# The first stage of a streaming encoder layer, reordered by token tile and weight quarter

## The reference, cut to what matters

```
xn = x * rsqrt(mean(x * x) + EPS) * g_mix_norm
z = xn @ w_in                       # 1024 x 3488
c_q, c_kv, k_r, u, gate_a, gate_b = split(z)   # 256 + 128 + 32 + 1024 + 1024 + 1024 columns
```

## Time and profile before

| | |
|---|---|
| median of three runs | 859.44 us (859.42 to 859.92) |
| the profiled execution | 859.77 us |
| its span | 857.5 us |
| TensorE busy | 841.3 us, 98% |
| VectorE, ScalarE, POOL busy | 572.4, 365.2, 199.1 us |
| first transpose, first latent product, item 0 (starts) | 5.38, 15.12, 39.49 us |

### The profile page before, as it was taken

How to read it: one execution, slowest core, us unless ns; L and a number is a source line. 1 busy time by engine, 2 the same in 40 slices (tenths; PEclk the granted TensorE clock), 3 DMA queues, 4 the chain that set the end, 5 groups by cost and what they waited for, 6 DMA issues and landing times.

```text
span 857.5 us, 16853 instructions
## 1 busy us (share of the span) xinstructions
PE 841.3 (98%) x6564; PEld 806.9 (94%) x6564; DVE 572.4 (67%) x1056; ACT 365.2 (43%) x608; POOL 199.1 (23%) x228
## 2 busy tenths in 40 slices
PE   7999999899999999999999999999999999999998
PEld 7999899789999899877999999999999999999998
DVE  5686678877676676887655888878888886222121
ACT  6635959755645556557245222222222221222121
POOL 4021123202111121121140444333442344010000
PEclk9999999999999999999999999999999999999999
DMA  8434211131120200100223233232323223233321
GB/s 256 112 91 109 78 51 39 40 81 38 33 58 18 53 26 28 50 2 26 75 75 99 74 99 92 79 98 73 98 79 92 86 79 93 83 106 103 105 57 40
DMA packets 114466, 63.73 MB, mean 74 GB/s; under 512 B 7660, under 2 KB 112878, under 8 KB 114412
## 3 DMA queue, kind: packets, MB, share of 16 engines
q1 hardware_dynamic: 112428, 59.25, 24.2%
q0 software_dynamic: 1936, 3.70, 1.7%
q10 hardware_dynamic: 48, 0.02, 0.0%
HBM read 59.85 MB, written 2.70 MB: 73 GB/s over the span
## 4 chain that ended last, share of the span: by engine, by line
PE 88%; ACT 6%; DVE 3%; issue 2%; DMA 0%; SPq 0%; ACTq 0%; DVEq 0%
PE PS L1632 49%; PE PS L1785 9%; PE PS L1868 6%; PE PS L1840 4%; PE PS L1802 4%; PE PS L1678 3%; PE PS L1744 2%; PE PS L1822 2%; PE PS L2075 2%; PE PS L1776 2%; PE PS L1740 1%; PE PS L1766 1%; PE PS L1707 1%; PE PS L1644 1%; PE PS L1847 1%
## 5 line engine op out<-in xcount | busy, mean ns | idle before, releaser
L682 ACT ACTIVATE w_hi<-w_raw 128x1024 fp32r<-128x1024 f32 (+2 forms) x102 | 105.4, 1034 | 301.4 <-PE PS L1632 288.8
L1115 DVE TENSOR_TENSOR w_lo<-w_raw,w_hi 128x1024 fp32r<-128x1024 f32 (+2 forms) x102 | 127.2, 1247 | 103.6 <-ACT w_hi L682 103.5
L1632 PE MATMUL PS<-x2h,w_hi 128*128 128x272 f32 x704 | 145.7, 288 | 0.0
L1632 PE MATMUL PS<-x2h,w_lo 128*128 128x272 f32 x704 | 145.7, 288 | 0.0
L1632 PE MATMUL PS<-x2l,w_hi 128*128 128x272 f32 x704 | 145.1, 288 | 0.0
L1632 PEld LDWEIGHTS PS<-x2h,w_hi 128*128 128x128 f32 x704 | 110.8, 188 | 0.1
L1632 PEld LDWEIGHTS PS<-x2l,w_hi 128*128 128x128 f32 x704 | 110.6, 189 | 0.0
L1632 PEld LDWEIGHTS PS<-x2h,w_lo 128*128 128x128 f32 x704 | 109.9, 189 | 0.0
L643 POOL TENSOR_TENSOR uct<-uct 128x512 f32<-128x512 f32 x22 | 28.4, 1292 | 165.0 <-DVE uct L1585 165.0
L1632 PE MATMUL PS<-hh,w_hi 128*128 128x272 f32 x308 | 64.2, 289 | 0.0
L1632 PE MATMUL PS<-hh,w_lo 128*128 128x272 f32 x308 | 63.8, 288 | 0.0
(11 more groups left out here) (295 smaller groups left out, 1865.1 us busy)
## 6 DMA issues: line engine op xcount, KB each, us to landing
w_raw<-in_w_up_dram SPq DMA_DIRECT2D x44, 512.0 KB, 3.8
w_raw<-in_w_in_dram SPq DMA_DIRECT2D x24, 512.0 KB, 3.8
w_raw<-in_w_down_dram SPq DMA_DIRECT2D x16, 512.0 KB, 3.6
w_raw<-in_w_out_dram SPq DMA_DIRECT2D x8, 512.0 KB, 3.6
w_raw<-in_w_down_dram SPq DMA_DIRECT2D x8, 384.0 KB, 3.9
xnat<-in_x_prompt_dram SPq DMA_DIRECT2D x4, 512.0 KB, 5.0
w_raw<-in_w_in_dram SPq DMA_DIRECT2D x4, 416.0 KB, 6.5
wq<-in_w_q_b_dram SPq DMA_DIRECT2D x8, 192.0 KB, 2.5
```

Of the source, the lines that this page charges most:

```text
L682: nc.scalar.activation(hi[:, slot % 2, 0:n], raw[:, slot % 4, 0:n], ACT.Copy).then_inc(s_hi, 1)
L1115: tt(lo[:, slot % 2, 0:n], raw[:, slot % 4, 0:n], hi[:, slot % 2, 0:n].bitcast(F32), ALU.subtract).then_inc(s_lo, 1)
L1632: last = mm(joined_half(2 * rank, j), w[:, slot % 2, cols], x[:, k0 + k, j * HT:(j + 1) * HT], start=(k0 + k == 0 and first), stop=(k0 + k ...
```

## The change

The tokens go through the first stage in seven parts (`XPARTS`): tiles 0 and 1 in halves of four feature blocks, the others whole. SP loads them so, with the four weight quarters between, and the small vectors behind all of them. For each part VectorE scales the transposed columns by the gain from PSUM into a buffer `xg` (`x_scaled`), ScalarE makes the high part from it (`x_hi`), VectorE the low part (`x_lo`). ScalarE copies each transposed tile to `xT` on its own (`x_kept`). The latent weight quarters are split into places of their own, `lw_hi` and `lw_lo`. TensorE's order is written out: transposes, latent products by tile and quarter (`latent_product`, six matmuls) and ten identity products in three groups. Tiles 1 and 3 are transposed into banks 6 and 7, the others into 0 and 1; tiles 3 and 4 accumulate in banks 6 and 7, so their first products also wait for the kept copy of tile 3. The splits of items 0 and 1 stand ahead of ScalarE's vector copy and exponential, and ahead of VectorE's softplus chain; the copy of `rsT` stands behind that chain.

```diff
+        xg = at("xg", [P, 2, KD, P], gates_at)
+        lw_hi = at("lw_hi", [P, 4, 2 * LAT], v_at + 4 * 2 * P * 4, F32R)
+        lw_lo = at("lw_lo", [P, 4, 2 * LAT], gates_at + 2 * KD * P * 4, F32R)
...
+        XPARTS = [(0, 0, 4), (0, 4, 8), (1, 0, 4), (1, 4, 8)] + [(t, 0, 8) for t in range(2, NTT)]
+        def parts_of(t):
+            return sum(part[0] <= t for part in XPARTS)
+        def part_with(t, k):
+            return [k0 <= k < k1 and tile == t for tile, k0, k1 in XPARTS].index(True)
+        def x_columns(t, k0, k1):
+            bank = 6 if t in (1, 3) else 0
+            return PS[:, bank:bank + 2, :].rearrange("p a (k n) -> p (a k) n", k=4)[:, k0:k1, 0:TOK[t][2]]
+        def x_tile(x, t, k0, k1):
+            c0, _, n = TOK[t]
+            return x[:, k0:k1, c0:c0 + n]
...
-            for t, (c0, p0, n) in enumerate(TOK):
-                src = i["x_prompt"][0, c0:c0 + n, :] if t < NT else i["x_sample"][0]
-                sp.dma_start(xnat[p0:, t, :], src).then_inc(s_xt[t], 16)
+            def load_x(t, d0=0, d1=D):
+                c0, p0, n = TOK[t]
+                src = i["x_prompt"][0, c0:c0 + n, d0:d1] if t < NT else i["x_sample"][0]
+                sp.dma_start(xnat[p0:, t, d0:d1], src).then_inc(s_xt[part_with(t, d1 // P - 1)], 16)
             def latent_weights(t):
                 sp.dma_start(raw[:, t, 0:2 * LAT].rearrange("p (k n) -> p k n", k=2),
                              w_in_k[:, 2 * t:2 * t + 2, 0:LAT]).then_inc(s_w[t], 16)
+            load_x(0, 0, D // 2)
             latent_weights(0)
+            load_x(0, D // 2, D)
+            load_x(1, 0, D // 2)
+            load_x(1, D // 2, D)
             latent_weights(1)
+            load_x(2)
+            latent_weights(2)
+            load_x(3)
+            load_x(4)
+            latent_weights(3)
...
-            latent_weights(2)
-            latent_weights(3)
...
-            pool.wait_ge(s_xt[NT], 16)
+            pool.wait_ge(s_xt[-1], 16)
...
-                if not isinstance(t, int) or t >= 2:
+                if not isinstance(t, int) or t >= I_IN + 2:
...
+            def x_hi(part):
+                t, k0, k1 = XPARTS[part]
+                act.wait_ge(s_xg, part + 1)
+                nc.scalar.activation(x_tile(xnh, t, k0, k1), xg[:, t % 2, k0:k1, 0:TOK[t][2]], ACT.Copy).then_inc(s_xgh, 1)
+            def x_kept(t):
+                act.wait_ge(s_xTd, parts_of(t))
+                nc.scalar.activation(x_tile(xT, t, 0, KD), x_columns(t, 0, KD), ACT.Copy).then_inc(s_xTa, 1)
+            def latent_split_hi(q):
+                act.wait_ge(s_w[q], 16)
+                nc.scalar.activation(lw_hi[:, q, :], raw[:, q, 0:2 * LAT], ACT.Copy).then_inc(s_hi, 1)
+            def squares(t):
+                _, p0, _ = TOK[t]
                 if t:
                     act.wait_ge(s_ss, t)
                 nc.scalar.activation(junk[p0:, :], xnat[p0:, t, :], ACT.Square, accum_out=small[p0:, 2, t:t + 1]).then_inc(s_ss, 1)
...
+            act.wait_ge(s_vecT, 1)
+            nc.scalar.activation(vec[:, 0:8], PS[:, 2, 0:8], ACT.Copy).then_inc(s_vec, 1)
+            x_hi(0)
+            latent_split_hi(0)
+            x_hi(1)
+            x_hi(2)
+            latent_split_hi(1)
+            x_hi(3)
+            x_kept(0)
+            x_kept(1)
+            x_hi(4)
+            latent_split_hi(2)
+            act.wait_ge(s_cpre, 1)
+            squares(0)
+            x_kept(2)
+            x_hi(5)
+            squares(1)
+            x_kept(3)
+            x_hi(6)
+            x_kept(4)
+            latent_split_hi(3)
+            for t in range(2, NTT):
+                squares(t)
+            split_hi(I_IN, I_IN, 32)
+            split_hi(I_IN + 1, I_IN + 1, 32)
             act.wait_ge(s_vecT, 2)
             nc.scalar.activation(vec[:, 8:V_ALL], PS[:, 2, 8:V_ALL], ACT.Copy).then_inc(s_vec, 1)
             act.wait_ge(s_vec, 2)
             nc.scalar.activation(la_s[:, :], vec[:, V_LAM:V_LAM + KD], ACT.Exp, scale=-1.0).then_inc(s_spe, 1)
-            split_hi(3, 3, 16, 2 * LAT)
-            split_hi(I_IN, I_IN, 32)
...
-            split_hi(I_IN + 1, I_IN + 1, 32)
...
+            def x_scaled(part):
+                t, k0, k1 = XPARTS[part]
+                n = TOK[t][2]
+                dve.wait_ge(s_xTd, part + 1)
+                gain = vec[:, V_GMIX + k0:V_GMIX + k1].unsqueeze(2).to_broadcast([P, k1 - k0, n])
+                tt(xg[:, t % 2, k0:k1, 0:n], x_columns(t, k0, k1), gain, ALU.mult).then_inc(s_xg, 1)
+            def x_lo(part):
+                t, k0, k1 = XPARTS[part]
+                dve.wait_ge(s_xgh, part + 1)
+                tt(x_tile(xnl, t, k0, k1), xg[:, t % 2, k0:k1, 0:TOK[t][2]], x_tile(xnh, t, k0, k1).bitcast(F32),
+                   ALU.subtract).then_inc(s_xgl, 1)
+            def latent_split_lo(q):
+                dve.wait_ge(s_hi, q + 1)
+                tt(lw_lo[:, q, :], raw[:, q, 0:2 * LAT], lw_hi[:, q, :].bitcast(F32), ALU.subtract).then_inc(s_lo, 1)
+            dve.wait_ge(s_vec, 1)
+            x_scaled(0)
+            x_lo(0)
+            latent_split_lo(0)
+            x_scaled(1)
+            x_scaled(2)
+            x_lo(1)
+            x_lo(2)
+            latent_split_lo(1)
+            x_scaled(3)
+            x_lo(3)
+            x_scaled(4)
+            x_lo(4)
+            latent_split_lo(2)
+            x_scaled(5)
+            x_lo(5)
+            x_scaled(6)
+            x_lo(6)
+            latent_split_lo(3)
             dve.wait_ge(s_ss, NTT)
             link(ts(small[:, 2, 0:NTT], small[:, 2, 0:NTT], 1.0 / D, EPS, ALU.mult, ALU.add))
             for t in range(NTT):
                 last = ts(dgx[:, t, :], ident[:, :], small[:, 3, t:t + 1], None, ALU.mult)
             last.then_inc(s_rsn, 1)
-            split_lo(3, 3, 2 * LAT)
-            dve.wait_ge(s_rsb, 1)
-            nc.vector.tensor_copy(rsT[:, 0:SEQ], PS[:, 0, :])
-            nc.vector.tensor_copy(rsT[:, S0:], PS[:, 1, 0:DEC]).then_inc(s_rs, 1)
             split_lo(I_IN, I_IN)
+            split_lo(I_IN + 1, I_IN + 1)
...
+            dve.wait_ge(s_rsb, 1)
+            nc.vector.tensor_copy(rsT[:, 0:SEQ], PS[:, 0, :])
+            nc.vector.tensor_copy(rsT[:, S0:], PS[:, 1, 0:DEC]).then_inc(s_rs, 1)
...
-            split_item(I_IN + 1)
...
-            def x_transpose(t):
+            def x_transpose(part):
+                t, k0, k1 = XPARTS[part]
                 _, p0, n = TOK[t]
-                pe.wait_ge(s_xt[t], 16)
+                pe.wait_ge(s_xt[part], 16)
                 if t >= 2:
+                    pe.wait_ge(s_xg, parts_of(t - 2))
                     pe.wait_ge(s_xTa, t - 1)
-                    pe.wait_ge(s_xTv, t - 1)
...
+                for k in range(k0, k1):
+                    last = nc.tensor.transpose(x_columns(t, k, k + 1)[:, 0], xnat[p0:, t, k * P:(k + 1) * P], ident[p0:, p0:])
                 last.then_inc(s_xTd, 1)
+            def keep_clock(bank, count):
+                for _ in range(count):
+                    mm(PS[:, bank, 0:P], ident[:, :], ident[:, :], start=True, stop=True)
             def vectors_transpose():
                 pe.wait_ge(s_rows, 16 * 13)
-                pe.wait_ge(s_xTa, NT)
-                pe.wait_ge(s_xTv, NT)
+                pe.wait_ge(s_vec, 1)
                 for a, (c0, n) in enumerate(((0, V_N), (V_N, 2 * NU), (V_N + 2 * NU, 2 * NU), (V_N + 4 * NU, 2 * NU))):
                     last = nc.tensor.transpose(PS[:, 2, c0:c0 + n], vrows[0:n, a, :], ident[0:n, 0:n])
                 last.then_inc(s_vecT, 1)
+            def latent_product(t, q):
+                w0 = TOK[t][0] - TOK[t][1]
+                if t in (3, 4):
+                    pe.wait_ge(s_xg, parts_of(3))
+                    pe.wait_ge(s_xTa, 4)
+                for kk in range(2):
+                    k = 2 * q + kk
+                    pe.wait_ge(s_xgl, part_with(t, k) + 1)
+                    pe.wait_ge(s_hi, q + 1)
+                    cols = slice(kk * LAT, (kk + 1) * LAT)
+                    for w, x in ((lw_hi, xnh), (lw_hi, xnl), (lw_lo, xnh)):
+                        if w is lw_lo:
+                            pe.wait_ge(s_lo, q + 1)
+                        last = mm(PS[:, 3 + t, 0:LAT], x[:, k, w0:w0 + P], w[:, q, cols],
+                                  start=(k == 0 and w is lw_hi and x is xnh), stop=(k == KD - 1 and w is lw_lo))
+                if t == NT:
+                    last.then_inc(s_used, 1)
+                elif q == 3:
+                    last.then_inc(s_latp, 1)
+            def x_rms_spread():
+                pe.wait_ge(s_rsn, 1)
+                for t, (c0, p0, n) in enumerate(TOK):
+                    dst = PS[:, 0, c0:c0 + n] if t < NT else PS[:, 1, 0:n]
+                    last = mm(dst, ones[:, :], dgx[:, t, p0:p0 + n], start=True, stop=True)
+                last.then_inc(s_rsb, 1)
             pe.wait_ge(s_ident, 16)
             pe.wait_ge(s_gain, 16)
...
```

(65 more changed lines are left out.)

3 lines of the change are left out of this document (removed).

## The result

The changed kernel takes 872.14 us (median of 4 executions, 871.53 to 872.37) where the kernel before took 859.68 in the same runs (859.42 to 860.18): a ratio of 1.0143, 95% interval 1.013 to 1.0155. It is 12.5 us slower. The profiled execution took 871.53, with a span of 869.3 against 857.5, so the two profiles differ by 11.8.

What follows compares the result with a forecast made beforehand. TensorE, busy 98%, bounds the kernel, so item 0's start decides. Early-start gain and waits leave TensorE 6.6 us later, the late copy adds 2.8: +9.4 on 859.4 gives 868.8, range 864.0 to 872.5.

Steps and rivals of the forecast that it cites:

- the two waits: TensorE idle before quarter 2's products of tile 0, 4.4 us lost, and before tile 3's first product, 4.2 lost.
- the two paths: Ahead of item 0: TensorE's latent products, ending at 46.1, and VectorE's copy of the spread inverse, ending at 48.9.
- The likeliest case: Whole kernel: item 0 starts at 48.9 instead of 39.49, +9.4 us, giving 868.8; chance 0.60.
- Step 1: Start of the first stage: first latent product at 7.95, its third matmul at 9.0 instead of 15.12, about 7.2 us gained.
- Step 2: After tile 0 quarter 0 and eight transposes: TensorE waits 1.0 us for VectorE's scaling and low parts of two halves.
- Step 3: Tile 0's quarter 2: its split stands behind tile 2's chain, low part at 21.5; TensorE loses 4.4 us.
- Step 4: Tile 3: transposed late, its first product needs its kept copy, done at 32.3; TensorE loses 4.2 us.
- Step 5: Rest of the latent products and spread: TensorE ends the stage at 46.1, 6.6 us later than 39.49.
- Step 6: VectorE's tail: spread-inverse copy behind item splits and softplus chain ends at 48.9; item 0 waits, 2.8 us lost.
- the clock falls in the waits: Rival: the wait at tile 2 brings 1.2 GHz back, 12 matmuls take 0.38, 2.2 us more, 871.0; chance 0.22.
- The links are cheaper: Rival: scaling, high, low, copy and quarter splits at half price, item 0 at 42.4, 862.3; chance 0.10.
- the elementwise pair keeps pace: Rival: not slower, at a quarter of the prices in steps 3 and 4 item 0 at 40.1, 860.0; chance 0.08.

Runs made afterwards that it cites:

- the three moves: Changed kernel with tile 3's transposes early, weight quarter 2's split early and the `rsT` copy ahead of the softplus chain; 860.76 us, 1.0017 of the kernel before.
- the run with tile 3 early: Changed kernel with tile 3's transposes ahead of tile 0's quarter 2 product, tile 4's behind tile 2's second product; 863.78 us.
- the run with quarter 2 early: Changed kernel with weight quarter 2's split ahead of tile 2's own chain on ScalarE and VectorE; 868.5 us, 1.0099 of the kernel before.
- the first fill run: Changed kernel with identity products in both long TensorE waits, 14 behind tile 2's transposes and 17 behind those of tiles 3 and 4; 870.36 us.

## Why the prediction was right, and what it had too small

The direction, the place, the two waits and the two paths held. The likeliest case, 868.8, was 3.3 us low, because it left the clock out. By its steps:

Step 1, the first product at 7.95: it came at 7.96. Step 2, a wait of 1.0: 0.84. Step 3, quarter 2's low part at 21.5: 21.70, with the wait released by ScalarE's high part and then by VectorE's low part, as said. Step 4, 4.45 from the start of tile 3's scaling to the end of its kept copy (27.85 to 32.3): 4.28 (30.18 to 34.46). The scaling of 1024 elements out of PSUM, for which no row existed and 1.21 was chosen, took 1.24. Step 5, TensorE done at 46.1: 51.0, but with both waits filled it starts its last product at 46.4. Step 6, the copy at 48.9: 50.93, behind the same splits (2.35) and softplus chain (5.4) as priced; and the rest after item 0 unchanged, 818.3 for 818.2.

What failed is the term left out of the likeliest case: latent matmuls at 0.19 apart after the waits. From 20.43 and from 34.55 they came 0.35 apart. The rival "the clock falls in the waits" was the result. Its price of 2.2 was near (2.0: twelve matmuls at some 0.35, where it had twelve at 0.38; by the run that fills the first wait alone and starts item 0 at 48.98, where the forecast had 48.9), and so was its statement that the second slow stretch is absorbed: filling the second wait gained nothing. Its argument against itself, that two matmuls break the first wait, was worth nothing here: the clock had fallen within the wait (0.82 granted over it, 0.50 from 20.43). By the Trainium skill, "TensorE: Matmul & The Clock Gate", section "HAM oscillation — how this bites in real kernels", a data wait between bursts makes the next burst start cold; both long waits of this trace agree (0.50 granted after 3.28 and 3.79 us). This rival had been given a chance of 0.22.

Item 0 accounts for 2.1 of the 3.3 us (50.99 for 48.9). The other 1.2: 0.3 because 818.3 us follow item 0 and the sum counted 818.0, from the chain's 39.49 on (by the instruction's start, 39.32, the rest grew by 0.1 only), 0.6 because the median lies above the profiled execution (872.14 and 871.53), 0.3 because the forecast added the shift to a median that lies below the profiled execution before (859.44 and 859.77). The range was drawn to take in the clock rival, 871.0, and so the measured time lies inside it, 0.4 below the upper end; that these 1.2 us did not carry it out is luck.

"The links are cheaper" and "the elementwise pair keeps pace" fell with the rows: each link took what the straight lines said, and tile 3's kept copy came 4.3 us after its transposes.

## What to carry to other kernels

When work is cut finer so that it can start early, write down for each engine what stands ahead of the operation that the next consumer waits for. Here 7 us of early start were lost to a few operations standing behind others, and moving one tile's transposes ahead gave back 8.4. When two paths end together, an edit that shortens only one of them shows nothing, so try them together before calling one harmless. And a new wait on TensorE is priced with the matmuls after it: here the first wait, 3.3 us, cost 2.0 more behind it, while what the second cost was hidden behind the other path.

## What was not expected of the hardware

How long a wait was did not by itself say whether the clock fell behind it. After 2.28 us it was granted 0.64 over the next 4.5 us in one run, while after 2.27 us in another, the same wait at the same place, it stayed full: this window of the run with only the second wait filled starts 0.4 before its item 0, and from there pairs of products came 0.25 apart, where in the first run they came 0.45 apart.

```profile
50.90:53.50 2.60, 2.23 (x17) 2.23 (x18) 2.53 (x9) 0.00 (x0) 0.00 (x0) 1.00 0.00 0
```

In the run of the three moves it fell behind a wait of 1.27 us, with one of 0.50 before it and 2.5 us at full clock between the two; in the run with tile 3 early behind waits of 2.41 and 0.69. But in the run with quarter 2 early, no slow matmul followed the wait of 1.39. Nor did the fall always come at the end of a wait. In that run, after 3.79 us, the first four matmuls came some 0.2 apart and the next ones 0.35 apart, at 0.50 of the clock, only from 31.5. So in these runs a wait of one to three microseconds on TensorE brought a slow stretch in some cases and not in others, and both waits of over 3 us brought one in every profile that has them. What decided it was not tried. The executions of the three moves (860.56 to 863.3) and of the first fill run differ with their mean granted clock; that the clock is all of their difference is not shown.
